# Later coefficients, split up weights, other places at the seam, and scores right behind value products

## The reference

```python
h = rmsnorm(x, norm_mix); z = h @ w_in                 # 512 pool channels, then q, k, v of 12 heads of 64
a = pool_mixer(z[:, :512]) @ w_up_pool                 # window means minus input, a 128x128 map per group
b = attention(z[:, 512:]) @ w_up_attn                  # 3 groups of 4 heads, windows +-64 at dilation 1, 4, 16
g = sigmoid(h @ w_gate + b_gate)
x = x + (g_a * a + g_b * b) @ w_out
h = rmsnorm(x, norm_ffn)
x = x + (silu(h @ w_ffn_gate) * (h @ w_ffn_up)) @ w_ffn_down
y = rmsnorm(x, norm_final)
```

## Time and profile before

| | us |
|---|---|
| median of 3 runs | 2647.15 (2644.4 to 2649.32) |
| the profiled execution | 2647.09 |
| its span | 2645.3 |
| PE busy | 2561.8 (97%) |
| PEld busy | 2069.8 (78%) |
| POOL busy | 1862.3 (70%) |
| DVE busy | 1228.6 (46%) |
| ACT busy | 1052.4 (40%) |
| mean granted clock of TensorE | 0.989 |

### The profile page before, as it was taken

The page is one execution under the profiler, slowest core; times in us unless marked ns, Lnnn a source line. Parts: engine busy times, 40 slices in busy tenths (PEclk is TensorE's granted clock), DMA queues, the critical chain, the costliest instruction groups (busy, mean ns, idle before and its releaser), DMA issues.

```text
span 2645.3 us, 33303 instructions
## 1 busy us (share of the span) xinstructions
PE 2561.8 (97%) x12048; PEld 2069.8 (78%) x12048; DVE 1228.6 (46%) x1673; ACT 1052.4 (40%) x2018; POOL 1862.3 (70%) x1358
## 2 busy tenths in 40 slices
PE   6999999999999999999889999999999999999998
PEld 5887777788788888878768877777888888888786
DVE  6753556554422222354767535565543222223545
ACT  5224554344433233334542345543444333333444
POOL 7775445535888888798857754455458889887985
PEclk8999999999999999999989999999999999999999
DMA  3444455462333333464243434554622333334533
GB/s 128 128 133 121 142 156 173 134 240 73 92 104 100 110 102 100 157 208 152 98 148 114 148 110 145 151 174 141 240 76 84 104 96 120 96 108 158 183 121 139
DMA packets 331858, 350.76 MB, mean 133 GB/s; under 512 B 30640, under 2 KB 242992, under 8 KB 330160
## 3 DMA queue, kind: packets, MB, share of 16 engines
q1 hardware_dynamic: 328240, 338.03, 40.8%
q10 hardware_dynamic: 3456, 10.60, 1.0%
HBM read 249.28 MB, written 99.29 MB: 132 GB/s over the span
## 4 chain that ended last, share of the span: by engine, by line
PE 81%; POOL 5%; DVE 5%; DMA 3%; ACT 3%; issue 2%; SPq 0%; ACTq 0%; DVEq 0%; POOLq 0%
PE ps L1029 26%; PE ps L1031 25%; PE ps L1030 25%; POOL t_lo L797 2%; PE ps L1067 1%; POOL R L924 1%; PE ps L1102 1%; PE ps L1082 1%; PE ps L1049 1%; DMA Uh<-sp_rows 1%; DVE pw L1925 1%; DMA d_raw<-d_rows 1%; DVE xb L1802 1%; POOL wo_lo L941 0%; DVE X L1792 0%
## 5 line engine op out<-in xcount | busy, mean ns | idle before, releaser
L1029 PE MATMUL ps<-S,t_hi 128*128 128x512 f32 (+1 forms) x2336 | 922.0, 395 | 18.3 <-POOL t_lo L797 7.3
L1031 PE MATMUL ps<-S,t_lo 128*128 128x512 f32 (+1 forms) x2336 | 905.8, 388 | 0.0
L1030 PE MATMUL ps<-S,t_hi 128*128 128x512 f32 (+1 forms) x2336 | 905.7, 388 | 0.0
L1029 PEld LDWEIGHTS ps<-S,t_hi 128*128 128x128 f32 x2336 | 440.7, 189 | 123.6 <-issue 24.1
L1031 PEld LDWEIGHTS ps<-S,t_lo 128*128 128x128 f32 x2336 | 440.4, 189 | 91.1
L1030 PEld LDWEIGHTS ps<-S,t_hi 128*128 128x128 f32 x2336 | 441.2, 189 | 84.1
L797 POOL TENSOR_TENSOR t_lo<-wraw,t_hi 128x512 fp32r<-128x512 f32 x190 | 247.3, 1302 | 235.1 <-ACT t_hi L1425 232.5
L797 POOL TENSOR_TENSOR t_lo<-wraw_ff,t_hi 128x512 fp32r<-128x512 f32 x220 | 286.3, 1302 | 85.6 <-ACT t_hi L1425 81.5
L1425 ACT CAST t_hi<-wraw_ff 128x512 fp32r<-128x512 f32 x220 | 136.7, 623 | 365.8 <-PE ps L1031 365.6
L797 POOL TENSOR_TENSOR t_lo<-R,t_hi 128x512 fp32r<-128x512 f32 x154 | 233.0, 1519 | 59.1 <-ACT t_hi L1425 59.1
L2066 DVE TENSOR_TENSOR d_lo<-d_raw,d_hi 128x512 fp32r<-128x512 f32 x154 | 179.4, 1169 | 197.6 <-ACT d_hi L1614 197.3
(11 more groups left out here) (168 smaller groups left out, 4041.0 us busy)
## 6 DMA issues: line engine op xcount, KB each, us to landing
d_raw<-d_rows SPq DMA_DIRECT2D x154, 256.0 KB, 3.2
d_rows<-act_f SPq DMA_DIRECT2D x110, 256.0 KB, 2.1
wraw<-w_in SPq DMA_DIRECT2D x44, 512.0 KB, 5.7
wraw_ff<-w_ffn_up SPq DMA_DIRECT2D x44, 512.0 KB, 4.7
R<-w_ffn_down SPq DMA_DIRECT2D x88, 256.0 KB, 3.1
sp_rows<-gst SPq DMA_DIRECT2D x80, 256.0 KB, 2.5
wraw_ff<-w_ffn_gate SPq DMA_DIRECT2D x40, 512.0 KB, 5.0
wo_raw<-w_out SPq DMA_DIRECT2D x36, 512.0 KB, 3.3
```

Of the source, the lines that this page charges most:

```text
L1029: nc.tensor.matmul(o_ps, w[0], r[0], start=begins, stop=False, skip_group_check=True)
L1030: nc.tensor.matmul(o_ps, w[0], r[1], start=False, stop=False, skip_group_check=True)
L1031: return nc.tensor.matmul(o_ps, w[1], r[0], start=False, stop=ends, skip_group_check=True)
```

## The change

Four groups of edits, the same order of work otherwise:

- The transposes of the coefficients stand behind product 120 instead of 118, the spreads behind 122 to 127. Coefficients and selector have 128 rows, of which GpSimd clears those of `coefT` first.
- The up weights are rounded and subtracted in two parts, rows 0 to 3 and 4 to 5.
- `scores` of a duo stand behind `prob_v` of the duo two before it, one product earlier; softmax and exponentials move with them.
- At the seam: output tiles of the first sequence end in the order 0, 2, 4, 6, 5, 7, 1, 3; stores have a semaphore per two tiles, so that tokens 6 and 7 are loaded behind two stores; their statistics and norms come ahead of the last products' end; pair 0 of the second sequence has other buffers; the transposes 21 to 23 stand ahead of the first leading product; the rope table lies where output tiles 5 and 7 stood and is waited for by the first rope job only; the last two output tiles are normed beside products 3 to 6.

```diff
-FINAL = (0, 2, 4, 6, 1, 3, 5, 7)
+FINAL = ((0, 2, 4, 6, 5, 7, 1, 3), (0, 2, 4, 6, 1, 3, 5, 7))
-SPREAD0 = MERGE0 + 2
+SPREAD0 = MERGE0 + 4
-        rope_cos, rope_sin, r_s = at("rope_cos", XR, [T]), at("rope_sin", XR + 8192, [T]), at("rope_t", WX + 12288, [H2])
+        rope_cos, rope_sin = at("rope_cos", XR + 20480, [T]), at("rope_sin", XR + 28672, [T])
-        g_odd, squares4 = at("g_odd", WX + 4096, [D]), at("squares4", WX, [D])
+        g_odd, squares4 = at("g_odd", WR, [D]), at("squares4", WR + 4096, [D])
+        def wraw_of(s, n):
+            return wraw_ff[1] if s and n == 0 else (wraw_front if n < FF0 else wraw_ff)[n % 2]
...
                 if s:
-                    sp.wait_ge(t_ready, due("t_ready", s, 0))
-                    load_pair(s, 0)
-                    sp.wait_ge(d_ready, due("d_ready", s, 0))
-                    sp.dma_start(g_odd[:, :], norm_final.partition_broadcast(P)).then_inc(godd_in, 16)
-                    sp.wait_ge(even_stored, due("even_stored", s, 0))
+                    sp.wait_ge(tiles_stored[0], due("tiles_stored0", s, 0))
                 load_tokens(s, 3)
                 if s:
-                    sp.wait_ge(x_in[3], due("x_in3", s, 2))
+                    sp.wait_ge(d_ready, due("d_ready", s, 0))
+                    load_pair(s, 0)
+                    sp.wait_ge(t_ready, due("t_ready", s, 0))
+                    sp.dma_start(g_odd[:, :], norm_final.partition_broadcast(P)).then_inc(godd_in, 16)
                     sp.wait_ge(prod_done, due("prod_done", s, 0))
                 load_pair(s, 1)
-                sp.wait_ge(tr_full, due("tr_full", s, 28))
+                if s:
+                    sp.wait_ge(tiles_stored[2], due("tiles_stored2", s, 0))
                 for dst, n in ((rope_cos, 0), (rope_sin, 1)):
...
+                if m == SPREAD0 + 1:
+                    clear_coefficients(s)
+            def clear_coefficients(s):
+                pool.wait_ge(o_full, due("o_full", s, N_DUOS))
+                for r in range(2):
+                    pool.wait_ge(o_stored[r], due(f"o_stored{r}", s, 12))
+                nc.gpsimd.memset(coefT[:, :].bitcast(F32), 0.0).then_inc(cT_zero, 1)
...
+                for a, rows in enumerate((slice(0, 4), slice(4, 6))):
+                    pool.wait_ge(wu_hi_ready, due("wu_hi_ready", s, 2 * j + a + 1))
+                    nc.gpsimd.tensor_tensor(wu_lo[r][:, rows, :], wu_raw[r][:, rows, :], wu_hi[r][:, rows, :].bitcast(F32),
+                                            ALU.subtract).then_inc(wu_ready, 1)
...
-                nc.tensor.matmul(ps[:, b, :], sel[0:24, 2 * g + q, :, :].rearrange("r h e -> r (h e)"), coefT[0:24, half(h)],
+                nc.tensor.matmul(ps[:, b, :], sel[:, 2 * g + q, :, :].rearrange("r h e -> r (h e)"), coefT[:, half(h)],
...
-                if 0 <= duo < N_DUOS and step == 0:
-                    scores(s, duo)
                 if 1 <= duo <= N_DUOS and step == 0:
                     prob_transposes(s, duo - 1)
                 if 1 <= duo <= N_DUOS and step == 1:
                     prob_v(s, duo - 1)
+                if -1 <= duo < N_DUOS - 1 and step == 1:
+                    scores(s, duo + 1)
...
+                    part_transposes(s, 0, range(21, 24))
                     leading_product(s, 0, 0)
                     leading_product(s, 0, 1)
+                    leading_rest(s, 0, 0)
+                    pair_product(s, 2, done=0)
                     leading_product(s, 0, 3)
-                    part_transposes(s, 0, range(21, 24))
-                    leading_rest(s, 0, 0)
                     part_transposes(s, 0, range(24, 28))
-                    leading_rest(s, 0, 1)
-                    pair_product(s, 2)
+                    leading_rest(s, 0, 1, done=2)
                     leading_rest(s, 0, 3)
...
                     operand_hi(s, 0)
+                    part_his(s, 0, range(18, 24))
                     operand_hi(s, 1)
-                    part_his(s, 0, range(18, 21))
+                    final_stats(s - 1, 4)
+                    final_stats(s - 1, 5)
                     operand_hi(s, 2)
                     operand_hi(s, 3)
-                    final_stats(s - 1, 4)
-                    final_stats(s - 1, 5)
-                    first_stats(s, 3)
+                    first_product(s, 0)
                     store_out(s - 1, 4)
                     store_out(s - 1, 5)
-                    final_stats(s - 1, 6)
-                    final_stats(s - 1, 7)
-                    part_his(s, 0, range(21, 24))
-                    first_product(s, 0)
                     part_his(s, 0, range(24, 28))
...
-                    if 0 <= duo < N_DUOS and step == 1:
+                    if 0 <= duo < N_DUOS and step == 0:
                         exp_duo(s, duo)
+                    if s and m in (3, 4):
+                        final_stats(s - 1, 3 + m)
+                    if o == 6 and k == 9 and s + 1 < SEQS:
+                        first_stats(s + 1, 3)
...
-                dve.wait_ge(tab_in, due("tab_in", s, 2))
+                    if s and m in (5, 6):
+                        final_norm(s - 1, 1 + m)
-                    if 0 <= duo < N_DUOS and step == 0:
-                        softmax_duo(s, duo)
+                    if -1 <= duo < N_DUOS - 1 and step == 1:
+                        softmax_duo(s, duo + 1)
+                    if o == 6 and k == 10 and s + 1 < SEQS:
+                        first_norm(s + 1, 6)
+                        first_norm(s + 1, 7)
...
-                    part_los(s + 1, 0, range(EARLY_DONE - 1, 21))
+                    part_los(s + 1, 0, range(EARLY_DONE - 1, 24))
                     final_norm(s, 4)
                     final_norm(s, 5)
-                    first_norm(s + 1, 6)
-                    first_norm(s + 1, 7)
-                    final_norm(s, 6)
-                    final_norm(s, 7)
-                    part_los(s + 1, 0, range(21, 28))
+                    part_los(s + 1, 0, range(24, 28))
```

127 lines of the change are left out of this document (69 added, 58 removed).

## The result

Five runs of the changed kernel gave a median of 2632.38 us (2626.18 to 2634.14), against 2647.15 before (five runs as well, not three): ratio 0.9943, 95% interval 0.9930 to 0.9957, so 14.8 us faster. The forecast was 29.9 us, with a range that ended at 2632, just short of the median. The kernel was timed once more in a later batch: 2629.24 us, ratio 0.9936 (0.9924 to 0.9949). Sign and most of the steps came out; half of the size did not.

A forecast was written before the change was run, and what follows sets the result against it. The prediction took the order of TensorE's instructions as the bound, with losses from waits, low clock and matmul starts over 0.226 us apart. Its terms summed to -29.9 us: 2647.1 - 29.9 = 2617.2 us, range 2607 to 2632.

The forecast's parts named there:

- Coefficients: Transposes two products later, behind product 120: TensorE's wait goes, -7.6 us, and the low clock behind it, -3.4.
- -7.6, -3.4, -4.8: Up to product 130: coefficient wait gone, low clock behind it gone, and spreads padded to 128 rows, in us.
- I add 0.5 a sequence: +1.0, bounds 0 and +6: End of the front: cost in us of the merge ending two products nearer to the up products.
- Padding: Coefficient spreads with 128 rows: 0.40 us saved on each of 12 pairs, -4.8 us, bounds 0 and -4.8.
- the 2.74 that I took as upper bound: GpSimd's clear of the padded coefficients: bounds 0 and 2.74 us, upper one taken, expected to be hidden.
- Scores: Attention stage, scores right behind value products: 0.15 us saved for 23 pairs in each sequence, -6.9 us, bounds 0 and -16.
- the whole 0.35 us of an excursion: Attention stage: cost of entering and leaving a small matmul form; saving it for all 46 pairs was the -16 us bound.
- The -1.2 for probabilities: Attention stage: present 2.6 us of TensorE waits for probabilities lose part, -1.2 us, bounds 0 and -2.6.
- The +1.0 for the sum v: Softmax ahead of window sums on VectorE makes v up to 1.7 us later: +1.0 us, bounds 0 and +3.5.
- Up weights: Up stage, weights in two parts: TensorE's wait for GpSimd shrinks, -2.0 us, bounds 0 and -2.2.
- Seam: Between the sequences: earlier token loads and rope table start product 5 sooner, -6.0 us, bounds 0 and -11.
- Product 5, forecast near 1358 us: Start in the second sequence, a sign of being right: 6 us earlier by the seam, 12 by the first sequence.

The follow-up runs named there:

- a_act: Changed kernel with ScalarE's rounding of the first merged group (m_hi) put ahead of its roundings of the up weights; 2622.50 us, ratio 0.9908.
- again: Second trace of the changed kernel, unedited, from a later batch; 2629.24 us, ratio 0.9936.
- a_half: Changed kernel with two of the four window-sum passes of the last two pooling jobs left out, means not the reference's; 2627.36 us, ratio 0.9926.
- a_tail: Changed kernel with VectorE's lower half of the first merged group (m_lo) moved behind the mix rows' lower halves; 2629.99 us, ratio 0.9934.

## Why the prediction was off, by its steps

1. **Coefficients.** The gain to product 130 was sized right: with the padding -15.8 measured, -15.8 forecast (-7.6, -3.4, -4.8). The step that failed is "I add 0.5 a sequence: +1.0, bounds 0 and +6", the price of a merge that ends two products nearer to the up products. The tail measured +10.8 in the profiled execution and +8.3 in the second, past even the bound. I had counted the work behind the last spread, but not what it waits for and who stands behind it: the weights' load waits for the last spread and moved with it; ScalarE rounds these weights first; VectorE's subtraction of m_hi stands ahead of the eviction that the next product needs; and after the idle time TensorE ran at 0.52 of full clock. The 0.9 us wait for gst in the earlier trace rows was this chain already, with two products more of cover. Of the 10.8 us, 5.4 are the longer wait for gst and 1.1 waits for v at product 131, so the bound of +6 (3 us late in each sequence) was about right for the waits; what it left out is the clock behind them, most of the other 4.3. a_act shows the cause: one rounding moved, and the tail costs 2.7 us.
2. **Padding.** The row was read right: 0.41 us a pair against the 0.40 of the forecast, in all six spread steps of the changed kernel (3.17 us a product with its pair of spreads, 3.59 before). Alone it measured -4.5, by an interval that would hold 3.5 as well. The clear takes 0.96 us, not the 2.74 that I took as upper bound; ScalarE's copy waits for it (4.3 us in two waits), TensorE does not. The Trainium skill's rule that a single matmul of 32 rows takes as long as one of 128 ("TensorE: Matmul & The Clock Gate", "Why this matters for your kernels") would have given 3.5 us. Two of 24 rows took 0.41 us more than two of 128, ways in and out included, 4.9 us for 12 pairs. No run here has single matmuls apart from those ways, so the rule itself is not tested.
3. **Scores.** The pairs gained 0.19 us against 0.15: -7.8 between products 20 and 109, -6.9 forecast. A free change between the two small forms would have saved the whole 0.35 us of an excursion, so there is a price there too; this agrees with the Trainium skill's "Changing tiling mode (not just tile) drains the TensorE" ("TensorEngine Tiling (Array Packing)", "Key Properties"). The -1.2 for probabilities did not come (2.6 to 2.3 us). The +1.0 for the sum v was mis-sized: products 109 to 112 lose 4.2 us in "again" and 5.7 in the profiled execution, where the clock fell in the second sequence too (0.89 over the 15.65 us, 1.00 over 14.20 in "again"), so the bound +3.5 was too small. I had moved the softmax ahead of the passes and charged its 1.7 us once. It comes in both sequences; it stands for scores that TensorE has only just made (3.69 us idle before it), so that the passes start 1.0 us ahead of product 109, and not 4.0 as in the second sequence before; the first pass then starts together with a GpSimd operation and takes 1.84 us in place of 0.71 (a_half above); and the idle time of TensorE can lower the clock.
4. **Up weights.** The up stage gained 2.6 us, 2.0 forecast, and the wait for wu_lo is gone. But the wait for gl, the gates, at the first output products rose from 1.2 to 2.9 us, against this row of before:

```profile
PE ps L1029 <- DVE gl L2024: 1.2, 1, 1.2
```

In the first sequence it is new and costs 1.4 of the 1.6 us that the stretch behind the up stage gives back. What arrives earlier waits for the gates; no run took this part alone.

5. **Seam.** 5.3 to 7.1 us by the ratios, 6.4 by the means of the traces, 6.0 forecast. Single traces gave -4.2 and -8.0 for the same program, so one alone would have misled. Product 5, forecast near 1358 us, came at 1368.75 and 1364.63, mostly because the first sequence had gained 4.9 and 5.3 us by its last stage, and not 12.

By terms, in the profiled execution, which gained 12.9 us of 29.9 (the medians 14.8): of the 17.0 us missing, 9.8 are the tail, 4.7 the window sums, 2.2 the stretches behind the up stage (1.4 of them the gates), 0.5 the seam and 0.3 the attention stage with its probabilities; the up stage itself gave 0.6 more than forecast. That a median of 2632.38 comes so near the end of the range is luck of a kind: the range went that far for a seam and moved scores that give nothing, and the seam and the pairs of units gave what was forecast.

## What to carry to other kernels

A moved step moves the release of its buffers, and so every load that waits for them; follow the load to the engine that stands for it, and look at what is queued behind that engine's wait. A small wait (0.9 us here) at the place that will lose cover was the most telling row of this case: it was the end of the chain that later cost most. Where a wait moved when its step was moved (a_tail), the cause sat one queue further up (a_act). And what is moved on VectorE can land beside GpSimd's work and take more than twice its time (0.71 to 1.84 us here), so both queues have to be read at the new place.

## What the runs showed of the hardware

- Two traces of the same program differ by 7.5 us at TensorE's end, most of it in steps of 1 to 4 us at places where TensorE had idled for some us (3.03 us at 1311, 3.1 us at product 132), with the granted clock at 0.5 to 0.7 in the one and 1.00 or a shorter stretch in the other. Ratios over several runs settle what such a trace can't.
- The same wait does not always lower the clock: behind 2.5 us of idle time at product 110 it fell in seven places of 14, behind 1.4 us in none of four.
- VectorE's operations with two inputs stretch beside GpSimd's. The 128x1024 subtraction took 1.21 us with GpSimd idle (495.58) and 1.58 to 2.02 us beside GpSimd's subtractions of the up weights; a window pass of 513 to 527 columns took 0.69 to 0.71 us with GpSimd idle and 1.64 to 1.84 beside it at product 109. When the two started within 0.01 us of each other, either one could be the longer: over all traces with the moved scores, 1.84 and 1.28 us in 20 places, 0.71 and 1.87 in four.
